# Turning a block of gathered expert rows as two 64-row halves into two PSUM banks

## The chip, the core and the metric

The kernel runs on one core of one Trainium2 chip. The metric is the device time of one execution in microseconds; for the kernel before it is the median of three runs.

## What is computed

A sequence of 1024 tokens of width 1024 goes through a two-layer block (attention or mLSTM mixer, then a mixture of experts, each with a layer norm) and then through a second two-layer block. The change touches the mixture of experts, which runs once in each of the two layers of the first block. Cut to what matters:

```python
def expert_block(args):
    xb, e = args                      # 128 gathered rows, one expert
    hb = jax.nn.silu(xb @ w_gate[e]) * (xb @ w_up[e])
    return hb @ w_down[e]
y = lax.map(expert_block, (buf.reshape(n_blocks, MOE_BLOCK, D), block_e))
```

`MOE_BLOCK` is 128, `D` 1024, there are 16 experts with an inner width of 512, and each token goes to two of them.

## The kernel before

`run_experts` is the expert stage. Its outer loop runs over the 16 experts; an inner loop with bounds read at run time (`pe.Fori(lo, hi)`) runs over the blocks of 128 rows of one expert. All float32 values are split into a high part and a rest ("low") in a reduced format, and each product is made of three matmuls (high times high, low times high, high times low).

For one block TensorE does, in this order: the gate product into one bank (lines 1851, 1852 and 1856, 512 columns each); the up product in two halves of 256 columns (the same lines), with the first half of the block's hidden values turned in between (`turn_hidden(i, 0)`, line 1865); then `turn_rows(i + 1)`, which turns the rows of the **next** block; then `turn_hidden(i, 1)`; then the down product (lines 1875, 1878, 1881). Everything is in one queue, in program order, held only by semaphores.

The rows of a block come by an indirect DMA from GpSimd (`gather`, line 1991) into the tile `e_rows`, 128 rows on 128 partitions. `turn_rows` (line 1840) makes eight transposes. Each takes as weights the 128 columns k, k+8, k+16, ... of all 128 rows, so with a step of eight values of four bytes, and as moving operand the 128x128 identity; it writes 128 columns into PSUM. Four of them fill bank 2, four bank 3:

```python
for k in range(KT):
    mm = pe.transpose(x_bank[k // 4][:, (k % 4) * P:(k % 4 + 1) * P], rows[:, k:D:KT], core.c["ident"])
```

ScalarE copies both banks into `e_rowsT_high` (line 1913, `rows_parts`), VectorE then subtracts it from the banks into `e_rowsT_low` (line 175, called from `rows_parts`). Both are weights of the next block's gate and up products. GpSimd waits for the transposes before it gathers the block after next. Before the loop `turn_rows(0)` turns the first block; TensorE has nothing else to do there. Weights of the next expert come by DMA from SyncE into a second set of tiles and are split by ScalarE, VectorE and GpSimd between their parts in the blocks.

Three other places of the program are spoken of below. In the neighbourhood attention, line 800 turns probabilities as 64-row halves into two banks. In the memory attention, line 937 multiplies on 64 partitions and line 947 turns 128x128 tiles. In the retention (second block), lines 2978 and 2997 multiply on 64 partitions, the two sides in turn, between matmuls on 128 partitions (line 309 before, lines 2983 and 3002 after). Line 1303 turns contiguous 128x128 tiles.

Of the kernel before, what the change touches and what calls it, by code (L numbers as in the profile page):

```python
# [12 lines left out]
ACT = mybir.ActivationFunctionType  # L13
AX = mybir.AxisListType

P = 128
D = 1024
SEQ = 1024
TILES = SEQ // P
KT = D // P  # L20
# [10 lines left out]
HEAD = 64  # L31
# [48 lines left out]
@contextmanager  # L80
def stage(nc, *names, until_here=()):

    sems = [nc.alloc_semaphore(f"{n}_{nc.next_id()}") for n in names]
    with nc.Block() as block:
        yield block, dict(zip(names, sems))
    nc.clear_and_free_semaphores(sems + list(until_here))
    nc.all_engine_barrier()
# [85 lines left out]
def leave_low(eng, low, whole, high):  # L173

    return eng.tensor_tensor(low, whole, high, ALU.subtract)  # L175
# [1585 lines left out]
def run_experts(nc, core, ids, bounds, parts, loaded, early, norm):  # L1761
# [16 lines left out]
    def high(e, part):  # L1778
        return (wide if part == DOWN else tall)[(3 * e + part) % len(RING)]
# [6 lines left out]
    def high_count(e, part, k):  # L1786
        return (3 * e + part) * PIECES + k // STEP[part] + 1

    def on_pool(part, k):
        return part == DOWN and k >= POOL_FROM  # L1790
# [8 lines left out]
    rows = m.at("e_rows", o, [P, D])  # L1799
    rows_high = m.at("e_rowsT_high", o + 4 * KB, [P, KT, P], F32R)  # L1800
    rows_low = m.at("e_rowsT_low", o + 8 * KB, [P, KT, P], F32R)
# [5 lines left out]
    g_bank, x_bank, y_bank = core.bank[0], core.bank[2:4], core.bank[5:7]  # L1807
    u_bank = [core.bank[1][:, 0:HALF], core.bank[7][:, 0:HALF]]
    h_bank = [core.bank[0][:, 0:HALF], core.bank[4][:, 0:HALF]]
    x_banks = core.psum[:, 2:4, :]  # L1810

    def end_of(eng, e):
        return eng.value_load(bounds[0:1, 1, e:e + 1], min_val=1, max_val=MAX_BLOCKS)

    with stage(nc, "index_ready", "index_seen", "rows_gathered", "rows_turned", "rows_high_ready", "rows_low_ready",
               "w_high_ready", "w_low_ready", "down_low_ready",
               "gate_ready", "up_ready", "gate_done", "hidden_ready", "hidden_turned", "hid_high_ready", "hid_low_ready", "out_ready",
               "out_copied0", "out_copied1", "out_stored", "out_free", *norm.SEMAPHORES,
# [1 line left out]
        @block.sync  # L1820
        def _(sp):
            for e in range(1, N_EXPERTS):
                if e == 1:

                    sp.wait_ge(s["rows_gathered"], 16)
                else:

                    sp.wait_ge(s["out_ready"], end_of(sp, e - 2) * 2 + 2)
                load_expert(sp, parts, e, loaded)
            sp.wait_ge(s["out_ready"], end_of(sp, N_EXPERTS - 2) * 2 + 2)  # L1830
            early.load(sp)
            norm.sync(sp, s)

        @block.tensor
        def _(pe):
            def turn_rows(i):

                pe.wait_ge(s["rows_gathered"], (i + 1) * 16)
                for k in range(KT):
                    mm = pe.transpose(x_bank[k // 4][:, (k % 4) * P:(k % 4 + 1) * P], rows[:, k:D:KT], core.c["ident"])  # L1840
                mm.then_inc(s["rows_turned"], 1)

            def enter(dst, e, part, cols, half_way=None):
# [42 lines left out]
            pe.sem_inc(s["hidden_turned"])  # L1886
            lo, hi = 0, end_of(pe, 0)
            turn_rows(0)
            for e in range(N_EXPERTS):
                after = end_of(pe, e + 1) if e + 1 < N_EXPERTS else None  # L1890
# [18 lines left out]
        @block.scalar  # L1909
        def _(act):  # L1910
            def rows_parts(i):
                act.wait_ge(s["rows_turned"], i + 1)
                act.activation(rows_high[:, :, :].rearrange("p (b k) q -> p b (k q)", b=2), x_banks, ACT.Copy).then_inc(s["rows_high_ready"], 1)

            def copy_before(i):

                act.wait_ge(s["out_ready"], 2 * i + 1)
                act.wait_ge(s["out_free"], i + 1)
                act.activation(y[:, 0:BANK], y_bank[0][:, :], ACT.Copy).then_inc(s["out_copied0"], 1)

            lo, hi = 0, end_of(act, 0)
            for e in range(N_EXPERTS):
                after = end_of(act, e + 1) if e + 1 < N_EXPERTS else None
                for j, k in slices:
                    if e == 0 and (j, k) == (UP, 0):
                        rows_parts(0)
                    if k == 0:
                        act.wait_ge(loaded[e % 2][j], 16 * (e // 2 + 1))
                    act.activation(high(e, j)[:, k:k + STEP[j], :], W[e % 2][j][:, k:k + STEP[j], :], ACT.Copy).then_inc(s["w_high_ready"], 1)  # L1929
                with act.Fori(lo, hi) as i:  # L1930
                    copy_before(i)
                    act.wait_ge(s["gate_ready"], i + 1)
                    act.wait_ge(s["hidden_turned"], 2 * i + 1)
                    act.activation(hid[:, :], g_bank[:, :], ACT.Silu).then_inc(s["gate_done"], 1)
                    for part in range(2):
                        act.wait_ge(s["hidden_turned"], 2 * i + 2 + part)
                        act.activation(hid_high[:, 2 * part:2 * part + 2, :].rearrange("p k q -> p (k q)"),  # L1937
                                       h_bank[part], ACT.Copy).then_inc(s["hid_high_ready"], 1)
                    rows_parts(i + 1)
                lo, hi = hi, after  # L1940
            copy_before(lo)
            act.wait_ge(s["out_ready"], 2 * lo + 2)
            norm.scalar(act, s)

        @block.vector
        def _(dve):
            def rows_parts(i):
                dve.wait_ge(s["rows_high_ready"], i + 1)
                leave_low(dve, rows_low[:, :, :].rearrange("p (b k) q -> p b (k q)", b=2), x_banks,
                          rows_high[:, :, :].rearrange("p (b k) q -> p b (k q)", b=2)).then_inc(s["rows_low_ready"], 1)  # L1950

            def copy_before(i):

                dve.wait_ge(s["out_ready"], 2 * i + 2)
                dve.wait_ge(s["out_free"], i + 1)
                dve.tensor_copy(y[:, BANK:D], y_bank[1][:, :]).then_inc(s["out_copied1"], 1)

            dve.sem_inc(s["hidden_ready"])
            lo, hi = 0, end_of(dve, 0)
            for e in range(N_EXPERTS):  # L1960
                after = end_of(dve, e + 1) if e + 1 < N_EXPERTS else None
                for j, k in slices:
                    if e == 0 and (j, k) == (UP, 0):
                        rows_parts(0)
                    if not on_pool(j, k):
                        dve.wait_ge(s["w_high_ready"], high_count(e, j, k))
                        leave_low(dve, low[e % 2][j][:, k:k + STEP[j], :], W[e % 2][j][:, k:k + STEP[j], :],
                                  high(e, j)[:, k:k + STEP[j], :]).then_inc(s["w_low_ready"], 1)
                with dve.Fori(lo, hi) as i:
                    copy_before(i)  # L1970
                    dve.wait_ge(s["gate_done"], i + 1)
                    for part in range(2):
                        half = slice(part * HALF, (part + 1) * HALF)
                        dve.wait_ge(s["up_ready"], 2 * i + 1 + part)
                        dve.tensor_tensor(hid[:, half], hid[:, half], u_bank[part], ALU.mult).then_inc(s["hidden_ready"], 1)
                        dve.wait_ge(s["hid_high_ready"], 2 * i + 1 + part)
                        leave_low(dve, hid_low[:, 2 * part:2 * part + 2, :].rearrange("p k q -> p (k q)"), h_bank[part],
                                  hid_high[:, 2 * part:2 * part + 2, :].rearrange("p k q -> p (k q)")).then_inc(s["hid_low_ready"], 1)
                    rows_parts(i + 1)
                lo, hi = hi, after  # L1980
            copy_before(lo)
            norm.vector(dve, s)
# [2153 lines left out]
```

## Time and profile before

| | us |
|---|---|
| median of three runs | 3326.69 (3325.76 to 3327.88) |
| the profiled execution, its own time | 3334.11 |
| its span, first to last instruction | 3332.4 |
| TensorE busy | 3124.0, 94% of the span |
| VectorE, ScalarE busy | 1869.1 (56%), 1326.2 (40%) |
| 16 DMA engines | mean busy share by slices, up to 0.9 |

PE is TensorE's matmul, PEld its weight load, which overlaps the matmuls. A matmul's record lasts longer than the step to the next one, because it is pipelined: its end is modelled. So busy shares near 100% say that TensorE never stood still for long, and the step from one start to the next says what an instruction costs.

### The profile page before, as it was taken

To read this page: it belongs to the slowest core of one execution; us is meant where nothing else is said; L and a number is where in the kernel's file an instruction comes from. 1 tells how busy PE (TensorE), PEld (TensorE's weight loads), DVE (VectorE), ACT (ScalarE), POOL (GpSimd) and SP (SyncE) were. 2 spreads that over 40 slices of the span, in tenths; PEclk is the share of its full clock that TensorE was granted. 3 is DMA by queue.
4 is the path that set the end of the run, shared out by engine and by line. 5 is a ranking of instruction groups with operands and counts; after the bars stand their busy time and mean duration, and the time that the engine had idled before them with its cause. 6 is when DMAs were issued, how large, how long until landed. Compare 5 with 4: busy or idle time off the path is not lost. (4 is left out here: it accounts for less than half of the span.)

```text
span 3332.4 us, 52582 instructions
## 1 busy us (share of the span) xinstructions
PE 3124.0 (94%) x20573; PEld 2515.4 (75%) x20573; DVE 1869.1 (56%) x3550; ACT 1326.2 (40%) x2419; POOL 395.9 (12%) x321
## 2 busy tenths in 40 slices
PE   7999997999999989979799999799989989999999
PEld 6896675888867767867588888488856678896567
DVE  5535747658647725774656556634366543435654
ACT  2006823648542134451356555411345430134442
POOL 0100201334330000020133324100000000000000
PEclk9999998999999989989899999899999999999999
DMA  7626325769866300012568667610000220100022
GB/s 224 162 69 176 133 95 204 304 274 388 330 245 180 115 22 1 25 40 102 214 248 333 271 243 292 235 34 27 26 17 1 108 103 21 39 26 17 1 75 90
DMA packets 204508, 459.28 MB, mean 138 GB/s; under 512 B 56355, under 2 KB 131447, under 8 KB 195577
## 3 DMA queue, kind: packets, MB, share of 16 engines
q1 hardware_dynamic: 185849, 389.04, 32.6%
q0 software_dynamic: 18432, 67.12, 5.3%
q8 instruction: 154, 2.52, 0.3%
q14 instruction: 73, 0.60, 0.1%
HBM read 381.17 MB, written 72.22 MB: 136 GB/s over the span
## 5 line engine op out<-in xcount | busy, mean ns | idle before, releaser
L1851 PE MATMUL psum<-high_in,e_rowsT_high 128*128 128x256 f32 (+1 forms) x1080 | 330.1, 324 | 5.4 <-DVE e_rowsT_low L175 5.4
L1852 PE MATMUL psum<-high_in,e_rowsT_low 128*128 128x256 f32 (+1 forms) x1080 | 326.4, 320 | 0.0
L175 POOL TENSOR_TENSOR low_down<-w_down,high_out 128x1024 fp32r<-128x1024 f32 x64 | 207.8, 3265 | 297.6 <-ACT high_out L1929 297.6
L1851 PEld LDWEIGHTS psum<-high_in,e_rowsT_high 128*128 128x128 f32 x1080 | 206.6, 191 | 22.3 <-issue 6.1
L1852 PEld LDWEIGHTS psum<-high_in,e_rowsT_low 128*128 128x128 f32 x1080 | 206.8, 191 | 16.2
L175 DVE TENSOR_TENSOR low_gate<-w_gate,high_in 128x1024 fp32r<-128x1024 f32 x128 | 148.0, 1218 | 7.4 <-ACT high_in L1929 7.0
L175 DVE TENSOR_TENSOR low_up<-w_up,high_in 128x1024 fp32r<-128x1024 f32 x128 | 147.9, 1217 | 0.0
L3783 DVE CUSTOM_DVE_ANT_0 mla_probs<-psum,mla_mask 128x512 f32<-128x512 f32 (+2 forms) x192 | 96.7, 554 | 72.8 <-PE psum L3654 62.8
L1856 PE MATMUL psum<-low_up,e_rowsT_high 128*128 128x256 f32 x720 | 130.5, 283 | 0.0
L1929 ACT ACTIVATE high_in<-w_gate 128x1024 fp32r<-128x1024 f32 x128 | 124.8, 1059 | 6.7 <-issue 6.7
L1929 ACT ACTIVATE high_out<-w_down 128x1024 fp32r<-128x1024 f32 x128 | 124.6, 1050 | 5.6 <-DMA w_down<-in_exp_w_down 5.5
L1929 ACT ACTIVATE high_in<-w_up 128x1024 fp32r<-128x1024 f32 x128 | 124.6, 1051 | 0.0
L157 ACT ACTIVATE proj<-psum 128x512 f32<-128x512 f32 (+2 forms) x32 | 16.9, 528 | 259.0 <-PE psum L309 220.3
L3824 ACT ACTIVATE mla_probs<-mla_probs,mla_low 128x256 f32<-128x256 f32 (+7 forms) x128 | 98.0, 767 | 50.8 <-DVE mla_low L3787 48.9
L159 DVE COPY proj<-psum 128x512 f32<-128x512 f32 (+2 forms) x32 | 19.3, 603 | 173.9 <-PE psum L309 173.3
L1937 ACT ACTIVATE e_hiddenT_high<-psum 128x256 fp32r<-128x256 f32 x90 | 34.6, 385 | 204.6 <-PE psum L1865 204.6
L1875 PE MATMUL psum<-high_out,e_hiddenT_high 128*128 128x512 f32 x360 | 115.4, 402 | 0.0
L303 PE MATMUL psum<-ring_high,s_x_high 128*128 128x512 f32 (+3 forms) x576 | 112.9, 338 | 0.0
L1878 PE MATMUL psum<-low_down,e_hiddenT_high 128*128 128x512 f32 x360 | 111.8, 392 | 0.0
L1881 PE MATMUL psum<-high_out,e_hiddenT_low 128*128 128x512 f32 x360 | 110.9, 389 | 0.0
L307 PE MATMUL psum<-ring_low,s_x_high 128*128 128x512 f32 (+3 forms) x576 | 110.6, 334 | 0.0
L309 PE MATMUL psum<-ring_high,s_x_low 128*128 128x512 f32 (+3 forms) x576 | 110.6, 334 | 0.0
(611 smaller groups left out, 7476.9 us busy)
## 6 DMA issues: line engine op xcount, KB each, us to landing
w_gate<-in_exp_w_gate SPq DMA_DIRECT2D x32, 2048.0 KB, 8.3
w_up<-in_exp_w_up SPq DMA_DIRECT2D x32, 2048.0 KB, 13.5
w_down<-in_exp_w_down SPq DMA_DIRECT2D x32, 2048.0 KB, 19.7
ada<-in_ada_w SPq DMA_DIRECT2D x24, 1024.0 KB, 7.8
expert_rows<-e_out POOLq DMA_DIRECT2D x47, 512.0 KB, 7.2
expert_rows<-zero_row SPq DMA_DIRECT2D x33, 512.0 KB, 6.9
token_rows<-x SPq DMA_DIRECT2D x32, 512.0 KB, 2.6
x<-token_rows SPq DMA_DIRECT2D x24, 512.0 KB, 6.8
```

Source lines behind the costliest of these rows:

```text
L175: return eng.tensor_tensor(low, whole, high, ALU.subtract)
L303: pe.matmul(dst, lhsT, rhs, start=(m == 0), stop=False)
L307: pe.matmul(dst, lhsT, rhs, start=False, stop=False)
L309: mm = pe.matmul(dst, lhsT, rhs, start=False, stop=(m == len(ops) - 1))
L1851: pe.matmul(dst, rows_high[:, k, :], w_high[:, k, cols], start=(k == 0), stop=False)
L1852: pe.matmul(dst, rows_low[:, k, :], w_high[:, k, cols], start=False, stop=False)
L1856: mm = pe.matmul(dst, rows_high[:, k, :], w_low[:, k, cols], start=False, stop=(k == KT - 1))
L1875: pe.matmul(dst, hid_high[:, k, :], w_high[:, k, cols], start=(k == 0), stop=False)
L1878: pe.matmul(dst, hid_high[:, k, :], w_low[:, k, cols], start=False, stop=False)
L1881: mm = pe.matmul(dst, hid_low[:, k, :], w_high[:, k, cols], start=False, stop=(k == HT - 1))
L1929: act.activation(high(e, j)[:, k:k + STEP[j], :], W[e % 2][j][:, k:k + STEP[j], :], ACT.Copy).then_inc(s["w_high_ready"], 1)
L3824: act.activation(row, row, ACT.Exp, bias=low[:, n, side:side + 1], scale=-1.0, accum_out=sums[:, p, i // 4, side, i % 4:i % 4 + 1]).then_i ...
```

## The change

`turn_rows` makes sixteen transposes in place of eight. For each k the upper 64 rows are turned into bank 2 and the lower 64 rows into bank 3; each takes 64 partitions by 128 columns as weights (with the same step of eight values), moves a 64x64 piece of the identity and writes 64 columns. The two of a pair use different halves of the array's rows and different banks. Bank 2 now holds the first 64 columns of all eight k, bank 3 the last 64, so the copy on ScalarE and the subtraction on VectorE address their tiles with one more dimension (2 x 8 x 64 in place of 1024 values in a row); they write the same tiles. A new semaphore `rows_seen` is raised by TensorE between the wait for the rows and the first transpose; nobody waits for it.

```diff
-    x_banks = core.psum[:, 2:4, :]
+    x_banks = core.psum[:, 2:4, :].rearrange("p h (k q) -> p h k q", q=HEAD)
+
+    def by_half(tile):
+        return tile[:, :, :].rearrange("p k (h q) -> p h k q", h=2)
...
                 pe.wait_ge(s["rows_gathered"], (i + 1) * 16)
+                pe.sem_inc(s["rows_seen"])
                 for k in range(KT):
-                    mm = pe.transpose(x_bank[k // 4][:, (k % 4) * P:(k % 4 + 1) * P], rows[:, k:D:KT], core.c["ident"])
+                    for half in range(2):
+                        part = slice(half * HEAD, (half + 1) * HEAD)
+                        mm = pe.transpose(x_bank[half][:, k * HEAD:(k + 1) * HEAD], rows[part, k:D:KT], core.c["ident"][part, part])
                 mm.then_inc(s["rows_turned"], 1)
...
-                act.activation(rows_high[:, :, :].rearrange("p (b k) q -> p b (k q)", b=2), x_banks, ACT.Copy).then_inc(s["rows_high_ready"], 1)
+                act.activation(by_half(rows_high), x_banks, ACT.Copy).then_inc(s["rows_high_ready"], 1)
...
-                leave_low(dve, rows_low[:, :, :].rearrange("p (b k) q -> p b (k q)", b=2), x_banks,
-                          rows_high[:, :, :].rearrange("p (b k) q -> p b (k q)", b=2)).then_inc(s["rows_low_ready"], 1)
+                leave_low(dve, by_half(rows_low), x_banks, by_half(rows_high)).then_inc(s["rows_low_ready"], 1)
```

TensorE's queue in the block loop, from the last matmuls of the up product to the first of the down product, before (the numbers behind the names are the program's):

```order
L1856 MATMUL psum<-low_up_157_7075,e_rowsT_high_7089 128x256 x4
L1838 ISA
L1840 MATMUL psum<-consts_49,e_rows_7088 128x128 x8
L1863 REGISTER_ALU
L1865 MATMUL psum<-consts_49,e_hidden_7094 128x128 x2
L1875 MATMUL psum<-high_out_7086,e_hiddenT_high_7091 128x512 x2
```

And the same place with the change; lines below the edit have moved by three to six.

```order
L1862 MATMUL psum<-low_up_157_7075,e_rowsT_high_7089 128x256 x4
L1841 ISA
L1846 MATMUL psum<-consts_49,e_rows_7088 128x64 x16
L1869 REGISTER_ALU
L1871 MATMUL psum<-consts_49,e_hidden_7094 128x128 x2
L1881 MATMUL psum<-high_out_7086,e_hiddenT_high_7091 128x512 x2
```

Nothing has moved; the eight transposes of 128 columns have become sixteen of 64, between the same neighbours, which use all 128 rows of the array.

## Rows read from the trace of the kernel before

**Rows 1.** Windows over both expert stages: busy by engine, clock, DMA share.

```profile
574.00:962.00 388.00, 387.64 (x2286) 341.35 (x2284) 249.63 (x280) 238.56 (x307) 144.11 (x100) 1.00 0.78 307
1648.00:2072.00 424.00, 423.15 (x2534) 377.89 (x2534) 256.92 (x293) 242.47 (x304) 140.33 (x100) 1.00 0.72 281
```

**Rows 2.** Instructions of one tile or line: ns least/median/most, first and last start.

```profile
L1840 PEld LDWEIGHTS psum<-consts,e_rows x376: 187/193/231, 566.0 to 2074.8; 128*128 128x128 f32 x188
L1303 PEld LDWEIGHTS psum<-consts,x x128: 138/140/143, 526.4 to 1609.2; 128*128 128x128 f32 x128
L800 PEld LDWEIGHTS psum<-consts,na_probs x768: 134/139/226, 279.4 to 392.7; 64*128 64x128 f32 x192
L2997 PEld LDWEIGHTS psum<-ret_state,ret_qsT x112: 182/188/188, 2267.5 to 2933.3; 64*128 64x128 f32 x112
L1865 PE MATMUL psum<-consts,e_hidden x180: 270/272/328, 583.0 to 2075.1; 128*128 128x128 f32 x180
```

**Rows 3.** Timeline (start, us), weight loads of the first and fifteenth turn in the loop.

```profile
584.04 0.97 PEld L1840 LDWEIGHTS psum<-consts,e_rows 128*128 128x128 f32 x8
...
836.32 0.97 PEld L1840 LDWEIGHTS psum<-consts,e_rows 128*128 128x128 f32 x8
```

**Rows 4.** Timeline of one block's turn and what follows.

```profile
655.74 0.65 PE L1856 MATMUL psum<-low_up,e_rowsT_high 128*128 128x256 f32 x4
...
656.22 1.06 PE L1840 MATMUL psum<-consts,e_rows 128*128 128x128 f32 x8
656.42 0.42 DVE L1975 TENSOR_TENSOR e_hidden<-e_hidden,psum 128x256 f32<-128x256 f32 x1
657.01 0.25 PEld L1865 LDWEIGHTS psum<-consts,e_hidden 128*128 128x128 f32 x2
657.12 0.38 PE L1865 MATMUL psum<-consts,e_hidden 128*128 128x128 f32 x2
...
658.87 1.22 DVE L175 TENSOR_TENSOR e_rowsT_low<-psum,e_rowsT_high 128x1024 fp32r<-128x1024 f32 x1 [0.49 <-ACT e_rowsT_high L1913]
...
662.61 0.19 PEld L1851 LDWEIGHTS psum<-high_in,e_rowsT_high 128*128 128x128 f32 x1
```

**Rows 5.** Timeline, neighbourhood attention: sixteen half transposes.

```profile
300.34 0.57 PEld L800 LDWEIGHTS psum<-consts,na_probs 64*128 64x128 f32 x16 [0.52 <-DVE na_probs L879]
300.34 0.71 PE L800 MATMUL psum<-consts,na_probs 64*128 64x64 f32 x16
300.98 0.63 PEld L836 LDWEIGHTS psum<-na_probsT,na_v 128*64 128x64 f32 x8
```

**Rows 6.** Timeline, retention: four pairs of matmuls on 64 rows.

```profile
2267.51 0.52 PEld L2997 LDWEIGHTS psum<-ret_state,ret_qsT 64*128 64x128 f32 x8 [0.27 <-issue]
2267.52 0.66 PE L2997 MATMUL psum<-ret_state,ret_qsT 64*128 64x64 f32 x8
```

**Rows 7.** Timeline, memory attention: 64-row matmuls, transposes, 64-row matmuls.

```profile
401.90 1.13 PE L937 MATMUL psum<-mem_kT,na_qm 64*128 64x256 f32 x8 [2.48 <-ACT ma_probs L1013]
402.96 0.86 PEld L947 LDWEIGHTS psum<-consts,ma_probs 128*128 128x128 f32 x8 [0.33 <-issue]
402.97 1.09 PE L947 MATMUL psum<-consts,ma_probs 128*128 128x128 f32 x8
403.99 0.30 PEld L937 LDWEIGHTS psum<-mem_kT,na_qm 64*128 64x128 f32 x4 [0.17 <-issue]
```

**Rows 8.** Timeline, before the first block of the first layer.

```profile
566.05 1.97 PE L1840 MATMUL psum<-consts,e_rows 128*128 128x128 f32 x8 [2.67 <-DMA e_rows<-token_rows,e_index]
...
568.06 1.02 ACT L1913 ACTIVATE e_rowsT_high<-psum 128x1024 fp32r<-128x1024 f32 x1 [3.26 <-PE psum L1840]
...
569.12 1.23 DVE L175 TENSOR_TENSOR e_rowsT_low<-psum,e_rowsT_high 128x1024 fp32r<-128x1024 f32 x1 [2.49 <-ACT e_rowsT_high L1913]
...
570.71 0.77 PE L1851 MATMUL psum<-high_in,e_rowsT_high 128*128 128x512 f32 x1 [2.68 <-DVE e_rowsT_low L175]
```

**Rows 9.** Instructions of line 903, a copy from two banks by halves.

```profile
L903 ACT ACTIVATE na_probsT<-psum x48: 1001/1024/1029, 280.9 to 393.1; 128x1024 f32<-128x1024 f32 x48
```

More of the change, by code:

```diff
@@ L1809, in run_experts @@
     h_bank = [core.bank[0][:, 0:HALF], core.bank[4][:, 0:HALF]]
-    x_banks = core.psum[:, 2:4, :]
+    x_banks = core.psum[:, 2:4, :].rearrange("p h (k q) -> p h k q", q=HEAD)
+    def by_half(tile):
+        return tile[:, :, :].rearrange("p k (h q) -> p h k q", h=2)
     def end_of(eng, e):
         return eng.value_load(bounds[0:1, 1, e:e + 1], min_val=1, max_val=MAX_BLOCKS)
-    with stage(nc, "index_ready", "index_seen", "rows_gathered", "rows_turned", "rows_high_ready", "rows_low_ready",
+    with stage(nc, "index_ready", "index_seen", "rows_gathered", "rows_seen", "rows_turned", "rows_high_ready", "rows_low_ready",
                "w_high_ready", "w_low_ready", "down_low_ready",
```

## The prediction

> **What bounds the kernel now.** First I read the busy time of the two expert stages by window [rows 1]. TensorE is busy for 387.64 of 388.00 us in the first and 423.15 of 424.00 us in the second, at a granted clock of 1.00 of full speed; VectorE has 64% and 61%, ScalarE 61% and 57%, the DMA engines 78% and 72%. So TensorE's queue sets the time here, and a longer or shorter turn is paid or gained in full as long as no other engine is waited for. A busy share can hide short waits, so I looked at the period next: the turn's weight loads start at 584.04 and, fourteen blocks later, at 836.32 [rows 3]; that is 252.28 / 14 = 18.02 us a block, on any expert, with one block or with two. A stage that waited for weights now and then would not be so even. The tile's row counts 376 loads on line 1840, which is 47 turns of eight; line 1865 has 180 matmuls, four a block, so 45 blocks [rows 2]. 45 turns stand in the loop, in TensorE's full queue, and 2 ahead of the loops.
>
> **One turn before.** The last up matmuls start at 655.74 and their records end at 656.39; the two transposes of the hidden values that follow the turn end at 657.12 + 0.38 = 657.50 [rows 4]. From the one end to the other 1.11 us pass. Inside, eight loads take 0.97 us, so with 0.19 us for one (median 193 ns) the step is (0.97 - 0.19) / 7 = 0.111 us [rows 2, 3]. Before the first load of the next group nothing stands still: it starts at 657.01, 0.27 us ahead of the modelled end of the turn's last matmul (656.22 + 1.06 = 657.28) [rows 4].
>
> **What a half transpose costs.** Three things are needed: the step from pair to pair, the cost of going from 128-row to 64-row work, and the cost of going back.
>
> The step. The trace has the same construct in the neighbourhood attention: sixteen loads of 64x128 take 0.57 us, (0.57 - 0.14) / 15 = 0.029 us for one and 0.06 for a pair [rows 5]. But it has contiguous columns there. Line 1303, also a transpose of contiguous columns, has a load of 140 ns; the experts' load, whose columns are eight values apart, has 193 ns; line 800's, contiguous, 139 ns [rows 2]. So I read the difference of 53 ns as the price of the step of eight, and nothing in the change takes it away: a half still reads 128 columns with the same step, only on fewer partitions. The nearest row for slow loads on 64 partitions in alternating halves is line 2997, whose load has 188 ns: eight loads in 0.52 us, (0.52 - 0.19) / 3 = 0.11 us from pair to pair [rows 2, 6]. Two loads on different halves do run side by side there, but a pair takes as long as one load of 128 partitions takes now. I take 0.11, since the load's duration is that of the experts' load to 5 ns. Bounds: 0.06 (line 800) and, if two strided loads went one after the other, twice 0.111 = 0.22.
>
> The Trainium skill, in SBUF — State Buffer, under Door 1: The DMA port swizzle, says that SBUF has lines of 16 bytes and that each access which crosses to a new one pays a penalty; eight float32 values are 32 bytes. The trace agrees, by 193 against 140 ns. In TensorE: Matmul & The Clock Gate, under LDWEIGHTS (loading the stationary operand), the skill says that a load's time goes by its columns, not by its partitions. That rule speaks against the change, and line 2997's row bears it out.
>
> The way in. In the memory attention TensorE goes from 64-row to 128-row work and back. Line 937's records end at 401.90 + 1.13 = 403.03, and line 947's first load starts at 402.96; line 947's end at 402.97 + 1.09 = 404.06, and the next load of line 937 starts at 403.99 [rows 7]. Both loads start 0.07 us ahead of the modelled end, where in the experts' loop it is 0.27. Line 800 ends at 301.05 and its successor starts at 300.98 [rows 5], 0.07 again. So at each such change of shape the next load is held back by 0.20 us. The neighbours of the turn use 128 rows, so two such changes come into each block, where there is none now. The skill's rule, in TensorEngine Tiling (Array Packing), under Key Properties, is that a change of the tiling mode drains the engine; the row and the rule agree, and the rule has no number.
>
> The way through. For four pairs line 2997 needs from its first load to the end of its last matmul 2268.18 - 2267.51 = 0.67 us [rows 6]; four pairs more make 0.67 + 4 x 0.11 = 1.11. Its matmuls are not transposes; those of line 800 end 0.05 us sooner after their load (0.57 + 0.14 = 0.71 us from the first load to the last end, of which seven steps of 0.061 are 0.43 and 0.28 the rest, against 0.67 - 0.33 = 0.34) [rows 5, 6]. I take 1.06.
>
> The sum of one turn, from the end of the up product's records: first load at -0.07, last end at 0.99, next load at 0.92, and two transposes of 128 columns after a change of shape take 0.45 us (line 947's eight take 404.06 - 402.96 = 1.10, less six steps of 0.11) [rows 7]: 1.37 us. Against 1.11 that is +0.26; the rows are rounded to 0.01 us, and several enter, so I take **+0.25 us a turn**. 45 turns make +11.2 us.
>
> **What is hidden or small.** Ahead of each layer's first block TensorE has only waited for rows (2.67 us idle), and works more slowly after it: eight transposes need 1.97 us [rows 8], where the loop's need 1.06 [rows 4]. The chain goes on through ScalarE's copy (568.06), VectorE's subtraction (569.12) and ends in the first matmul (570.71), so all of it counts. The excess is 1.97 - 1.06 = 0.91 us, 0.11 us a transpose, so the step has doubled to 0.22. A half moves half as many columns, and a pair may keep the load's 0.11. That would save seven steps of 0.11; my estimate is 0.7 us gained, twice: -1.4 us, bounds 0 and -1.5.
>
> The copies with one more dimension: line 903 copies 1024 values from two banks by halves in 1024 ns [rows 9]; the one on line 1913 takes 1.02 us [rows 8]. For the subtraction the trace has no such row. It ends at 658.87 + 1.22 = 660.09 and is first needed at 662.61 [rows 4], so even at twice its time (2.4 us) it stays covered by the down product; without that cover it would cost what it exceeds 1.22 by. The hidden values' product on VectorE ends at 656.84, before 657.01, and is now needed later [rows 4]. The new semaphore instruction stands where TensorE drains anyway; I take nothing, at most 0.05 us a turn, half a load's step of 0.11.
>
> Sum: 11.2 - 1.4 = +9.8 us. The profiled execution becomes 3334.11 + 9.8 = 3343.9 us; it stands 7.4 us above the median of the runs, and so I carry the difference over: 3326.69 + 9.8 = **3336.5 us**, 0.29% slower. A measurement of this kernel tells about 0.2%, 6.7 us, from no change.
>
> **Rivals.**
> Fast loads (not slower). If the 193 ns were not a matter of the step, the pairs would follow at 0.06 as on line 800: 0.71 us through, so 0.64 + 0.45 - 0.07 = 1.02 against 1.11, -0.09 a turn, 45 times, and -1.4: -5.5 us, 3321. VectorE's product at 656.84 allows at most 0.17 us of it. It decides from a pair step below 0.08. For it: the construct and its row; against: the load's duration.
>
> Full gain. Fast loads and no price for the change of shape: sixteen steps of 0.029 in place of eight of 0.111, -0.42 us a turn, of which VectorE's product lets 0.17 through: -7.7 - 1.4 = -9 us, 3317.5. The skill's table under Theoretical Speedup in TensorEngine Tiling (Array Packing) names up to twice the speed for a small dimension of 64. Against it: all three changes of shape in rows 5 and 7.
>
> No price for the change of shape here, slow loads: 1.11 becomes 1.11, only the first turns gain; -1.4 us, 3325. For it: those rows stand at phase starts with waits of their own. Against: line 1840 also starts with a wait and has no gap.
>
> Loads one after the other. 0.22 a pair: 8 x 0.11 = +0.88 more a turn, 1.13 in all, +51 us less 1.4: 3376. Against it: line 2997 and line 800 run side by side.
>
> **How the numbers follow.** Chances: forecast 0.70, fast loads 0.15, full gain 0.03, no price 0.07, one after the other 0.05. The forecast's own range: 0.20 a turn (if part of the hold is lost in rounding) to 0.35 (with 0.05 for the semaphore and 0.05 for matmuls as long as line 2997's), so +7.6 to +15.8 us, 3334 to 3342. The range over all takes in no price and fast loads: 3319 to 3342, leaving out the full gain, the loads in series and a rest. Slower: the forecast and the loads in series, 0.74 (a little of the forecast is within 0.2%, a little drift the other way evens it). Faster: the full gain and a third of the fast loads, 0.08. Same: the rest, 0.18.
>
> **What would show it.** In the changed profile: line 1846's weight loads x752, median near 190 ns (right) or 140 (fast loads); sixteen loads in about 0.97 us, or 0.57; next load 0.07 us ahead of the up product's end and of the turn's end; a period of 18.27 us in place of 18.02; line 1919 still near 1.02 us. Wrong it would be if the two halves' strided reads disturb each other, if the semaphore holds TensorE longer, or if the period's growth is taken back by a wait that TensorE now has and the busy share hides.

## The result and the profile after

| | before | with the change |
|---|---|---|
| median, us | 3327.88 (5 runs, 3325.76 to 3330.52) | 3345.45 (5 runs, 3341.05 to 3346.66) |
| ratio | | 1.0044, interval 1.0033 to 1.0056 |
| the profiled execution, its span | 3334.11, 3332.4 | 3345.45, 3343.8 |

The kernel is slower, as forecast, by 0.44%: 14.6 us (11.0 to 18.6). The forecast was +9.8 us. The median lies 3.5 us above the upper end of the range, so the direction was right and the size too small. The two medians are 17.6 us apart, more than the 14.6 of the ratio but within its interval: the size of the miss is itself uncertain by a few us.

I read the period of a block first, since the whole forecast hung on it. The timeline of the kernel with the change, weight loads of line 1846 (before: line 1840), the first turn of the loop and the fourteenth, start and length in us:

```profile
587.85 0.96 PEld L1846 LDWEIGHTS psum<-consts,e_rows 64*128 64x128 f32 x16
...
825.41 0.96 PEld L1846 LDWEIGHTS psum<-consts,e_rows 64*128 64x128 f32 x16
```

Between them lie 13 blocks: 237.56 / 13 = 18.27 us, where it was 18.02 [rows 3]. That is +0.25 us a block, the term of the prediction. The tile's instructions with the change, in ns least/median/most:

```profile
L1846 PEld LDWEIGHTS psum<-consts,e_rows x752: 182/202/207, 569.9 to 2083.9; 64*128 64x128 f32 x188
L1846 PE MATMUL psum<-consts,e_rows x752: 270/271/369, 570.0 to 2084.0; 64*128 64x64 f32 x188
```

The load of half the partitions takes 202 ns, no less than the full one's 193 [rows 2]. One block of the timeline with the change, to be laid beside [rows 4]:

```profile
587.29 0.64 PE L1862 MATMUL psum<-low_up,e_rowsT_high 128*128 128x256 f32 x4
...
587.85 0.96 PEld L1846 LDWEIGHTS psum<-consts,e_rows 64*128 64x128 f32 x16
587.86 1.10 PE L1846 MATMUL psum<-consts,e_rows 64*128 64x64 f32 x16
587.96 0.42 DVE L1980 TENSOR_TENSOR e_hidden<-e_hidden,psum 128x256 f32<-128x256 f32 x1
588.88 0.20 PEld L1871 LDWEIGHTS psum<-consts,e_hidden 128*128 128x128 f32 x2
588.88 0.44 PE L1871 MATMUL psum<-consts,e_hidden 128*128 128x128 f32 x2
...
589.64 1.02 ACT L1919 ACTIVATE e_rowsT_high<-psum 128x1024 fp32r<-128x1024 f32 x1
...
590.69 1.23 DVE L175 TENSOR_TENSOR e_rowsT_low<-psum,e_rowsT_high 128x1024 fp32r<-128x1024 f32 x1 [0.49 <-ACT e_rowsT_high L1919]
```

Sixteen loads take 0.96 us, so the step from pair to pair is (0.96 - 0.20) / 7 = 0.11. The first load starts 0.08 us ahead of the modelled end of the up product (587.93), and the next load of line 1871 0.08 ahead of the turn's end (588.96); before, the latter was 0.27. From the end of the up product to that of the hidden transposes (589.32) pass 1.39 us, 1.11 before. The copies on ScalarE and VectorE kept their 1.02 and 1.23 us.

That accounts for 45 x 0.254 = 11.4 us. The first turns give back less than I took (below), so some 4 us are missing. I looked for them stage by stage; most of the program's stages agree within the scatter, but two in the second layer of the second block do not. Windows laid around these two stages, TensorE alone (length, busy, granted clock, DMA share, GB/s); the kernel before:

```profile
2732.00:3016.60 284.60, 277.73 (x1636) 0.99 0.13 41
3016.60:3072.70 56.10, 52.75 (x768) 1.00 0.10 25
```

And with the change:

```profile
2740.00:3025.00 285.00, 277.85 (x1636) 0.99 0.13 41
3025.00:3084.20 59.20, 54.44 (x768) 0.97 0.10 24
```

From its first instruction to the end of its last the one stage lasts 283.5 us before and 284.5 after, the other 56.4 and 59.6, with the same instructions in the same number: +1.0 and +3.2, together +4.2 us, far from any line that the diff touches. Inside the second stage, the timeline before:

```profile
3022.03 4.14 PE L3306 MATMUL psum<-mla_w_uq,mla_qlT 128*128 128x384 f32 x12 [1.08 <-DMA mla_w_uq<-in_w_uq]
```

With the change:

```profile
3031.85 5.83 PE L3311 MATMUL psum<-mla_w_uq,mla_qlT 128*128 128x384 f32 x12 [2.58 <-DMA mla_w_uq<-in_w_uq]
```

TensorE waits for the weights `mla_w_uq` 1.50 us longer, and then the same twelve matmuls take 1.69 us longer: a window over them shows a lower granted clock, 0.70, where before it was 1.00. Before, then with the change:

```profile
3022.00:3026.10 4.10, 4.08 (x14) 1.00 0.43 79
```

```profile
3031.85:3037.60 5.75, 5.75 (x12) 0.70 0.02 4
```

What delays the transfer stands in the DMA view of the nine microseconds in which it runs. Before, from 3016.6:

```profile
q8 instruction: 1, 0.02, 0.8%
...
mla_w_uq<-in_w_uq SPq DMA_DIRECT2D x1, 768.0 KB, 4.5
```

With the change, from 3025.0:

```profile
q8 instruction: 2, 0.03, 1.7%
...
mla_w_uq<-in_w_uq SPq DMA_DIRECT2D x1, 768.0 KB, 6.0
```

Queue q8 carries TensorE's instructions (the experiments below lengthen TensorE's program alone, and its packets grow in number). With the window narrowed to the transfer itself, from issue to landing, the view has no q8 line before and two packets with the change: before, the one packet starts 4.9 us after the issue, behind the landing at 4.5; with the change they start at 1.8 and 5.8 us, and the transfer lands at 6.0. On the whole page that queue has (queue: packets, MB, share)

```profile
q8 instruction: 157, 2.57, 0.3%
```

and before it had 154 packets. The change makes TensorE's program longer: the turn stands 34 times in it (16 experts and one ahead of the loop, in two layers), each with 8 more loads, 8 more matmuls and a semaphore instruction, 34 x 17 = 578 instructions. From this came the second theory: **the place at which an instruction packet falls**, not the turn, makes the +4 us.

### The profile page after: what moved, and what is told of

It reads as the page before. It is cut to its first block and busy times, and to the rows that moved or that the text cites. A ratio compares the mean times of both kernels' runs of the same rounds, so it can differ in the third digit from the quotient of the medians.

```text
span 3343.8 us, 53381 instructions
## 1 busy us (share of the span) xinstructions
PE 3137.9 (94%) x20949; PEld 2521.2 (75%) x20949; DVE 1870.1 (56%) x3550; ACT 1327.3 (40%) x2419; POOL 400.8 (12%) x321
## 5 line engine op out<-in xcount | busy, mean ns | idle before, releaser
L175 DVE TENSOR_TENSOR e_hiddenT_low<-psum,e_hiddenT_high 128x256 fp32r<-128x256 f32 x90 | 38.2, 425 | 135.3 <-ACT e_hiddenT_high L1943 135.3
```

## The experiments

The first theory (A): strided half loads are as slow as full ones, and two changes of shape cost 0.20 us each. Its rivals: the period grows for another reason (the semaphore, the order of the halves). The second (B): the rest comes from the length of the program; its rival is mere scatter from execution to execution. The table gives each kernel's ratio to the kernel before with its interval, the period, and the sum of the two late stages named above, each from its first instruction to the end of its last (before 283.5 + 56.4 = 339.9, with the change 344.1).

| kernel | ratio | period, us | two late stages, us | q8 packets |
|---|---|---|---|---|
| ctl_before | 1.0004 (0.9995 to 1.0013) | 18.02 | 340.0 | 154 |
| rep_after | 1.0048 (1.0034 to 1.0062) | 18.27 | 343.9 | 157 |
| contig_full | 1.0012 (1.0003 to 1.0021) | 17.97 | 339.9 | 154 |
| contig_half | 1.0014 (1.0005 to 1.0023) | 17.90 | 344.3 | 157 |
| pad_before | 1.0026 (1.0015 to 1.0037) | 18.02 | 343.9 | 157 |
| pad_after | 1.0042 (1.0029 to 1.0056) | 18.27 | 340.1 | 157 |
| pad_even | 1.0005 (0.9996 to 1.0014) | 18.02 | 340.0 | 156 |
| before_seen | 1.0012 (1.0003 to 1.0021) | 18.02 | 343.7 | 155 |
| split_turn | 1.0091 (1.0076 to 1.0107) | 18.62 | 339.9 | 157 |
| in_series | 1.0119 (1.0103 to 1.0134) | 18.77 | 343.8 | 157 |
| half_step4 | 1.0056 (1.0042 to 1.0070) | 18.36 | 343.7 | 157 |
| half_step2 | 1.0058 (1.0045 to 1.0072) | 18.35 | 344.9 | 157 |

### The two kernels again (ctl_before, rep_after)

No edit but a blank line at the end.

> The kernel before again, nothing changed, as a control. Theory (the change acts only through the period of the expert blocks, and the rest of the difference between the medians is scatter from one execution to the next): ratio within 0.2% of 1, period 18.02 us, and its profiled stages outside the block loops differ from those of the first profile by single microseconds either way. Rival (the profiles of before and after differ outside the loops because of the change): stages outside the loops repeat the first profile of before to 0.3 us.

> The changed kernel again. Theory (45 turns at +0.25 us): period 18.27 us again, ratio 1.003 to 1.004, that is +10 to +13 us. Rival (a part of the cost lies outside the expert stages): +15 us or more, and the same stages are longer again.

The control is at 1.0004, and the change again at 1.0048, 16 us, the rival's outcome. The two late stages repeat to 0.2 us in each, so they are no scatter. Other stages do scatter: the neighbourhood attention took 123.5 us in the profiled execution with the change and 121.9 in its repeat, and in kernels built from the one before it took 121.4 to 123.5. The ends of the expert stages scatter too, where the results are gathered: from the last turn to the next stage pass 68.4 and 63.0 us in the two layers before, 63.8 and 60.5 with the change, but 69.8 and 63.9 in its repeat. So the two expert stages as a whole are only 2.7 us longer with the change in the first pair of profiles and 8.7 in the second (rep_after against ctl_before); the 11.4 us are read from the period alone. Two profiled spans can't be subtracted to a few us.

### Contiguous columns (contig_full, contig_half)

The turn reads 128 adjacent columns; the weights' rows are laid out to match, which cuts their transfers into 2 KB pieces. The output stays the same. In the kernel before:

```diff
-    srcs = [...rearrange("e (k p) n -> e p k n" if part == "down" else "e (p k) n -> e p k n", p=P)
+    srcs = [...rearrange("e (k p) n -> e p k n", p=P)
...
-  mm = pe.transpose(x_bank[k // 4][...], rows[:, k:D:KT], core.c["ident"])
+  mm = pe.transpose(x_bank[k // 4][...], rows[:, k * P:(k + 1) * P], core.c["ident"])
```

contig_half is the same edit in the changed kernel (`rows[part, k * P:(k + 1) * P]`).

> Kernel before with eight full transposes, but with contiguous columns (128 in a row) as weights; the gate and up weights are loaded in the matching layout, in pieces of 2 KB in place of 16 KB, so the output is the same. Theory (the step of eight values makes the load slow, the matmul of 128 columns hides nearly all of it): load median near 140 ns in place of 193, step 0.108 in place of 0.111, period 18.00, total -1 us, or more time if the DMA of small pieces is waited for. Rival (193 ns has another cause): the load stays near 193.

> Changed kernel with contiguous columns, the weights loaded as in contig_full. Theory (the strided load alone keeps a pair at 0.11 us; two changes of shape cost their 0.25 us in any case): load near 140 ns, a pair every 0.06 us, sixteen loads in 0.57 us, period 18.27 - 7 x 0.05 = 17.92 to 17.95, total 4 to 6 us under the kernel before. Rival (pairs are held at 0.11 by something other than the source's step): period 18.27, total +11 us.

The tile's loads in contig_half, in ns:

```profile
L1846 PEld LDWEIGHTS psum<-consts,e_rows x752: 134/138/226, 569.2 to 2079.3; 64*128 64x128 f32 x188
```

And its turn in the timeline:

```profile
587.00 0.59 PEld L1846 LDWEIGHTS psum<-consts,e_rows 64*128 64x128 f32 x16
587.00 0.72 PE L1846 MATMUL psum<-consts,e_rows 64*128 64x64 f32 x16
587.65 0.20 PEld L1871 LDWEIGHTS psum<-consts,e_hidden 128*128 128x128 f32 x2
```

With contiguous columns a pair takes (0.59 - 0.14) / 7 = 0.06 us, as on line 800 [rows 5], and the sixteen halves end at 0.72 us; the step of the columns thus carries the price of a half, as theory A says. The eight full loads in contig_full:

```profile
583.82 0.90 PEld L1840 LDWEIGHTS psum<-consts,e_rows 128*128 128x128 f32 x8
```

They still need 0.90 us: (0.90 - 0.14) / 7 = 0.11 from one to the next, with a load of 140 ns as with one of 193. So for full transposes the load's duration doesn't set the step of 0.11, and there the prediction's reading of it was too simple; for the halves it does. The period shows the whole trade: 17.97 to 17.90 with contiguous columns, 18.02 to 18.27 with the step of eight. Yet neither kernel gains. A timeline of contig_half behind an ordinary block shows why:

```profile
635.29 3.90 ACT L1935 ACTIVATE high_out<-w_down 128x1024 fp32r<-128x1024 f32 x4 [2.49 <-DMA w_down<-in_exp_w_down]
...
639.58 0.59 ACT L1940 ACTIVATE e_hidden<-psum 128x512 f32<-128x512 f32 x1
640.28 0.42 DVE L1980 TENSOR_TENSOR e_hidden<-e_hidden,psum 128x256 f32<-128x256 f32 x1 [0.94 <-ACT e_hidden L1940]
640.76 0.20 PEld L1871 LDWEIGHTS psum<-consts,e_hidden 128*128 128x128 f32 x2 [1.37 <-DVE e_hidden L1980]
```

ScalarE waits 2.49 us for the down weights, its next work is late, VectorE's after it, and TensorE waits 1.37 us. The down weights' own pieces haven't changed; they are issued behind those of gate and up. From issue to landing, w_gate takes 10.2 us in the median in contig_half and 9.8 in contig_full, 8.7 in the kernel before. In the profiled executions, blocks longer than the period lose 6.3 us in contig_half and 7.5 in contig_full, against 1.6 in the kernel before and 3.8 in ctl_before; contig_half gains 45 x 0.12 = 5.4 us, and has the +4 us of the late stages.

### Columns four and two apart (half_step4, half_step2)

The change with columns four (two) values apart, and weights in pieces of 8 KB (4 KB). The output stays the same.

```diff
-  mm = pe.transpose(..., rows[part, k:D:KT], core.c["ident"][part, part])
+  mm = pe.transpose(..., rows[part, k // STEP_IN * STEP_IN * P + k % STEP_IN:(k // STEP_IN + 1) * STEP_IN * P:STEP_IN], core.c["ident"][part, part])
```

> Changed kernel with columns four values apart (16 bytes) as weights in place of eight; gate and up weights are loaded in the matching layout, pieces of 8 KB, so the output is the same. Theory with the skill's lines of 16 bytes (each value still lies in a line of its own): load near 200 ns, a pair every 0.107 us, period 18.27. Rival (what is slow is a step over 16 bytes): load 138 ns, a pair every 0.062, period 17.9, total about 5 us under the kernel before plus what its longer program costs (4 us).

> The same with columns two values apart (8 bytes), pieces of 4 KB. Theory (two values lie in each line): load 138 to 150 ns, a pair every 0.06 to 0.07 us, period 17.90 to 17.95, where no block waits for its weights; total near the kernel before. Rival (only contiguous columns are fast): period 18.27, total as the changed kernel, +15 us.

half_step4, then half_step2, loads in ns:

```profile
L1851 PEld LDWEIGHTS psum<-consts,e_rows x752: 192/215/218, 569.7 to 2092.6; 64*128 64x128 f32 x188
```

```profile
L1851 PEld LDWEIGHTS psum<-consts,e_rows x752: 191/213/220, 569.8 to 2096.9; 64*128 64x128 f32 x188
```

Steps of 8, 4, 2 and 1 value give 202, 215, 213 and 138 ns. Each step over one that was tried is slow, and the smaller ones are no better than eight: half_step2's theory failed and its rival held. The periods, 18.36 and 18.35 us, are even 0.09 and 0.08 longer than with a step of eight, which neither expectation had; the sixteen loads of half_step4 take 1.03 us, so a pair every (1.03 - 0.22) / 7 = 0.116 us. That fits a pair's step that goes with its loads' duration. In the prediction I set the 53 ns beside the rule of the Trainium skill, SBUF — State Buffer, Door 1: The DMA port swizzle, that crossing to a new 16-byte line costs. By it a step of two values (8 bytes) would cross half as often and be cheaper. It is not: the measurement decides, and for weight loads that reading falls.

### The order of the halves (in_series)

```diff
-                for k in range(KT):
-                    for half in range(2):
+                for half in range(2):
+                    for k in range(KT):
```

> Changed kernel with the order of the two loops swapped: all eight transposes of the upper half, then all eight of the lower, the same instructions. Theory (the halves of a pair run side by side, that is why sixteen cost no more than eight): now each load of 128 strided columns costs its 0.11 us alone, +0.88 us a block, period 19.1 to 19.2, about +39 us over the changed kernel. Rival (loads do not overlap anyway): period 18.27.

The turn's loads:

```profile
588.03 1.46 PEld L1846 LDWEIGHTS psum<-consts,e_rows 64*128 64x128 f32 x16
589.56 0.20 PEld L1871 LDWEIGHTS psum<-consts,e_hidden 128*128 128x128 f32 x2
```

Sixteen loads one after the other would need 15 x 0.11 + 0.20 = 1.85 us; it is 1.46, and the period grows by 0.50 in place of 0.88. The trace's single starts fall into two series of eight, each with steps near 0.11 us: one from 588.035 to 588.786, the other from 588.535 to 589.292. The trace doesn't name the halves; that the second series is the lower half, which stands behind all eight of the upper one in the program, is my reading. By it the first load of the lower half starts between the upper half's at 588.456 and 588.566, before loads that are ahead of it in the queue, and the two series overlap for a quarter of a microsecond. The direction of theory A holds (pairs side by side save time), its size for "one after the other" was too high.

### Two more changes of shape (split_turn)

The turn in two groups: four pairs of it before the second half of the up product, four at the old place. That doubles the changes of shape. The wait for the rows and the instruction that raises `rows_seen` stand ahead of each group, so they are executed twice a turn.

```diff
+                    turn_rows(i + 1, range(KT // 2))
                     enter(u_bank[1], e, UP, ...)
-                    turn_rows(i + 1)
+                    turn_rows(i + 1, range(KT // 2, KT))
```

> Changed kernel with the sixteen half transposes in two groups of eight, one ahead of the second half of the up product and one at the old place: the same work, two changes of shape more in each block. Theory (changes of shape cost the time): +0.25 us a block again, period 18.5, about +11 us over the changed kernel. Rival (the sixteen transposes themselves are dear, or the semaphore): period 18.27 to 18.3.

```profile
583.93 0.52 PEld L1846 LDWEIGHTS psum<-consts,e_rows 64*128 64x128 f32 x8
...
587.79 0.52 PEld L1846 LDWEIGHTS psum<-consts,e_rows 64*128 64x128 f32 x8
```

The next turn's first group starts at 602.53, so this period is 18.60 us (18.62 in most blocks), +0.35 over the undivided turn, somewhat more than the 0.2 to 0.25 forecast. Ratio 1.0091, 0.0043 or some 14 us over rep_after. The transposes are the same sixteen, so the cost goes with the number of changes of shape; the second semaphore instruction isn't separated from it, but one alone costs nothing in the loop (next section).

### The semaphore alone (before_seen)

```diff
                 pe.wait_ge(s["rows_gathered"], (i + 1) * 16)
+                pe.sem_inc(s["rows_seen"])
```

in the kernel before, with `rows_seen` declared.

> Kernel before with the new semaphore instruction alone, ahead of the eight full transposes (34 instructions more). Theory (it is done while the matmuls ahead still run): the period stays 18.02, total within 0.15%. Rival (it holds TensorE's next load): period 18.05 to 18.1, +1 to +4 us.

The period stays at 18.02: the semaphore costs nothing in the loop, as taken. But these 34 instructions alone bring +3.8 us in the late stages (343.7), and the ratio of 1.0012 is 4 us. The change without its semaphore was not tried.

### Length of the program alone (pad_before, pad_after, pad_even)

Matmuls of one column and one row in a free bank, behind each layer's last block; their results are not used. 72 a layer in the kernel before (576 instructions in all, nearly the 578 of the change), 24 a layer in the changed one (192 more), and 64 a layer in the kernel before (512).

```diff
+            for n in range(72):
+                pe.matmul(core.bank[7][0:1, BANK - 1:BANK], core.c["ones"][:, 0:1], core.c["ones"][:, 0:1], start=True, stop=True)
             norm.tensor(pe, s)
```

> Kernel before with 72 tiny matmuls (1x1, results unused; each a weight load and a matmul in two passes, so 288 instructions) on TensorE behind the last block of each layer, where it waits for the gather of the results anyway: nearly as many instructions more in the program as the change adds (34 places x 17 = 578). Theory (the change has a second cost that has nothing to do with the turn: instruction packets of 16 KB are fetched at other moments, one of them inside the load of mla_w_uq in the second block): period 18.02, but the load of mla_w_uq in the second layer of the second block lands after about 6 us in place of 4.5 and its stage takes 59 us in place of 56; in all +3 to +5 us. Rival (the half transposes cause it in another way): 4.5 us and 56 us as before, total within 0.1%.

> Changed kernel with 24 such matmuls a layer (96 instructions, 192 in all): with the 578 of the change that is 770, three packets of 256 instructions and 2 more, so that the packets fall as in the kernel before. Theory (fetch): load of mla_w_uq lands after 4.5 us, its stage is back at 56 us, period stays 18.27, total 3 to 4 us under the changed kernel. Rival: the stage stays at 59 us.

> Kernel before with 64 in place of 72 tiny matmuls behind the last block of each layer: 512 instructions in all, exactly two packets of 256, at the same place and of the same kind as in pad_before. Theory (only where the packets fall counts): the stage with mla_w_uq is back at 56 us, its load lands after 4.5 us, the stage before it in the same layer is at 283.6, and the total is within 0.1% of the kernel before. Rival (any added instructions or the tiny matmuls themselves cost): ratio 1.002 to 1.003, as pad_before.

512 instructions make exactly two packets more (156), so one carries 256, and then all later packets should fall at the same instructions as before. This is the sharp test: pad_even is at 1.0005, mla_w_uq lands after 4.5 us, and the late stages are back at 340.0. In the DMA view of pad_even and of pad_before, nine microseconds around the transfer, pad_even's first:

```profile
q8 instruction: 1, 0.02, 0.9%
...
mla_w_uq<-in_w_uq SPq DMA_DIRECT2D x1, 768.0 KB, 4.5
```

```profile
q8 instruction: 2, 0.03, 1.6%
...
mla_w_uq<-in_w_uq SPq DMA_DIRECT2D x1, 768.0 KB, 5.8
```

pad_before, with 64 more instructions than pad_even and nothing else, is slower: 1.0026, late stages 343.9. The ratios are 0.0021 or 7 us apart, and their intervals (up to 1.0014, from 1.0015) hardly part; the late stages make 4 us of it. With pad_after they are back at 340.1 in the changed kernel, whose period stays 18.27. Its time (1.0042) can't be told from rep_after's (1.0048): 4 us is 0.12%, within both intervals. Theory B stands on the stages and on pad_even against pad_before; on whole times of the changed kernel it isn't shown.

All fourteen traces agree with it. In the six whose late stages take 340 us, no packet starts between the issue of `mla_w_uq` and its landing; in the eight with 344 to 345 us, one or two do. split_turn is a check that nobody planned: its program is longer than that of the change by one more semaphore instruction at each place in the loop, its first packet starts 5.5 us after the issue, behind the landing, and its late stages take 339.9 us. So it isn't the length as such. Why a packet of 16 KB holds a transfer of 768 KB back, so that TensorE's first matmul with it starts 0.9 to 1.7 us later, isn't shown.

How the 4 us split over the two stages follows TensorE's clock. In the first stage TensorE waits near the start for VectorE, which waits for the weights `ring`. Before, with the change, and in pad_before:

```profile
2745.92 6.39 PE L268 MATMUL psum<-ring_high,s_x_high 128*128 128x512 f32 x27 [1.81 <-DVE s_x_high L170]
```

```profile
2754.36 5.92 PE L268 MATMUL psum<-ring_high,s_x_high 128*128 128x512 f32 x25 [2.79 <-DVE s_x_high L170]
```

```profile
2754.64 7.61 PE L268 MATMUL psum<-ring_high,s_x_high 128*128 128x512 f32 x25 [3.32 <-DVE s_x_high L170]
```

The window 2755.50:2760.00 falls into these matmuls in the last two; with the change, then pad_before:

```profile
2755.50:2760.00 4.50, 4.50 (x22) 1.00 0.35 104
```

```profile
2755.50:2760.00 4.50, 4.50 (x14) 0.62 0.41 124
```

With the change the wait costs +1.0 us; in pad_before the clock falls behind it to the lower of its two levels (1.2 of 2.4 GHz) for some 3.4 us, and the first stage grows by 2.7. In the second stage it is the other way round. pad_before:

```profile
3033.59 4.14 PE L3308 MATMUL psum<-mla_w_uq,mla_qlT 128*128 128x384 f32 x12 [2.31 <-DMA mla_w_uq<-in_w_uq]
```

Its wait of 2.31 us is not followed by slow matmuls (4.14 us as before) and costs +1.2; with the change the wait of 2.58 us was, and cost +3.2. half_step4 and in_series go like pad_before, before_seen and contig_half like the change, and in half_step2 the clock falls in both stages, +5.0 us in all. In the first stage `ring` lands later (9.2 us in pad_before, 8.6 with the change, 8.0 before), but a packet starts before its landing in the kernels without the +1.0 us too, only later (7.2 to 7.6 us after the stage's start in place of 6.0 to 6.1), save split_turn, which has none there. So the packet's part is less clear in that stage than in the second.

## Why the forecast had the direction and missed the size

**The bound.** Right: TensorE's queue in the expert stages; a longer turn was paid in full. A few blocks wait in either kernel, 0.57 and 1.06 us in the execution before, 0.92 in that with the change (its row has 0.71 <-DVE e_hidden). It differs between executions of one kernel (3.8 us in four blocks of ctl_before), and the even period of the fourteen blocks I took hid it from my reading "on any expert".

**Loads as slow as full ones.** Right: 202 ns forecast near 190, sixteen in 0.96 us forecast 0.97. The reason, the column step, was right by contig_half; the smaller steps show that it isn't the number of lines crossed. What was too simple is that a load's duration sets the step: for full transposes it doesn't (contig_full), for pairs of halves it does.

**The way in and back.** Right: 0.08 us ahead of the modelled end on both sides, forecast 0.07, where it was 0.27, so the next load is held back by 0.19. The rule that a change of the tiling mode drains the engine (the Trainium skill, TensorEngine Tiling (Array Packing), Key Properties) agrees with split_turn, where two more changes in a block cost 0.35 us, for which I had 0.2 to 0.25.

**The sum of one turn.** +0.25 forecast, 0.254 measured; 45 turns are 11.4 us against 11.2. From the first load to the last end the halves take 1.11 us (588.96 - 587.85), where I took 1.06; line 2997's row alone would have given the 1.11; the whole stretch is 1.39 us against 1.37.

**The first turns.** The turn itself was right: from its first load to the first product 3.90 us against 4.66, -0.76. What I didn't see is that more than half of it is given back: TensorE runs at the lower of its two clock levels there (0.5 of full speed, 1.2 GHz), and the product that follows started sooner but stayed at it for longer. Windows over the first products, TensorE's granted clock in the third place, before:

```profile
570.00:575.00 5.00, 4.29 (x11) 0.52 1.01 429
575.00:580.00 5.00, 5.00 (x31) 1.00 0.98 408
```

And with the change:

```profile
575.00:580.00 5.00, 5.00 (x16) 0.60 1.02 434
580.00:585.00 5.00, 5.00 (x36) 1.00 0.97 398
```

From the first product's start, its matmuls reach the upper level with the eleventh before (574.98, 4.27 us later) and the thirteenth after (579.06, 5.21 us), which costs 0.94 us less the 0.46 that two matmuls take at the upper level, 0.48 us. The stretch from the first turn's start to the loop's first, over the profiled executions with the old turn and a step of eight (5) and with the new one (3), is 18.00 and 17.91 us in the first layer, 18.18 and 17.90 in the second; with the 0.19 of the hold that this stretch takes in, the two first turns gain 0.8 us, not 1.4. In the second layer it scatters between 17.5 and 18.7.

**The step that failed.** The sum, 11.2 - 1.4 = +9.8 us, took every cost to lie inside the expert stages, and so put at nothing, without a reason, what the longer program costs elsewhere. It counted the 16 added instructions of a turn as work of the engine, not as program that has to be fetched. With 578 instructions more, packets of 16 KB fell into the transfer of `mla_w_uq`: some +4 us in two late stages (4.2 in the first pair of profiles, 4.0 in the second), in a layer that the diff doesn't touch. The profile's page had the queue (154 packets), and nothing in the prediction read it. The smaller error is the term of the first turns, -1.4 us, which measured -0.8. With both, 11.4 - 0.8 + 4.0 = 14.6 us, where the ratio gives 14.6 (11.0 to 18.6). That the two agree so well is luck: the interval is wide, and 9.8 + 4.0, without the second correction, would lie in it as well. The forecast's own range reached +15.8 us, but by 0.35 us a turn, where 0.254 was measured; this cost wasn't in it.

**The base.** I took the median of three runs, 3326.69; that of five in the comparison was 3327.88. The forecast is compared with a median that lies 1.2 us above its own base. The 7.4 us that I took from the profiled execution to the median tell nothing of the change: the same kernel's median was 3336 to 3337 us in the other comparisons, and only the ratio carries over.

**The rivals.** Fast loads and full gain fall by 202 ns; no price for the change of shape by the hold; one after the other by the 0.96 us.

## What to carry to other kernels

Where the columns of a transpose's weights were strided and TensorE's queue was full, splitting it into row halves gained nothing (a pair still took 0.11 us), and each change of shape cost the queue about 0.2 us; only with contiguous columns did a pair become cheaper (0.06). Before summing a change, count the instructions that it adds to the program wherever the code is unrolled, and look at which transfers on a critical path an instruction packet can fall into. Where a few us are to be explained, compare stage by stage in repeated executions, and test a suspected program-length effect with padding that is a whole number of packets.

## What the runs showed of the hardware

- TensorE's instructions come in packets of 256 (512 more made two packets more). With one or two of them inside a 768 KB transfer it landed after 5.8 or 6.0 us in place of 4.5. TensorE's longer wait (2.58 in place of 1.08 us) was followed by twelve matmuls at a granted clock of 0.70, 1.69 us more; in pad_before a wait of 2.31 us was not.
- Float32 weight loads with columns 2, 4 or 8 values apart all take 202 to 215 ns, contiguous ones 138, at 64 partitions; at 128 partitions 193 and 140.
- Two series of loads on 64 rows, one behind the other in the program, overlap in time: the second starts at 588.535, between two loads of the first at 588.456 and 588.566. That the series are the two halves is read from their spacing.
- Pairs of half loads follow each other by 0.06 us with contiguous columns and 0.11 with a step of eight; full loads by 0.11 us with either (0.90 and 0.97 us for eight).
